# Memory attention woven between the q and output products, its two matrix products done in high and low parts

## The reference, cut to what matters

```python
def memory_cross_attention(h, mem_n, w_q, w_kv, w_o):
    q = (h @ w_q).reshape(B_, S_, MEM_HEADS, MEM_HEAD_DIM)
    kv = (mem_n @ w_kv).reshape(B_, M, 2, MEM_HEADS, MEM_HEAD_DIM)
    s = jnp.einsum('bshd,bmhd->bhsm', q, kv[:, :, 0]).astype(jnp.float32) * MEM_HEAD_DIM ** -0.5
    p = jax.nn.softmax(s, axis=-1).astype(h.dtype)
    o = jnp.einsum('bhsm,bmhd->bshd', p, kv[:, :, 1]).reshape(B_, S_, D_MODEL)
    return o @ w_o
```

## Time and profile before

| what | value |
| --- | --- |
| median of 3 runs | 3990.57 us (3990.21 to 3991.8) |
| profiled execution, its own time | 3986.77 us |
| span of its trace | 3985.5 us |
| TensorE busy | 3638.2 us, 91% of the span |
| VectorE, ScalarE, GpSimd busy | 51%, 37%, 38% |
| attention of layer 0 (first score to first matmul of the output product) | 451.66 to 498.86 us |
| the same in layer 1 | 1288.42 to 1337.18 us |

### The profile page before, as it was taken

The page is one execution under the profiler, slowest core; times in us unless marked ns, Lnnn a source line. Parts: engine busy times, 40 slices in busy tenths (PEclk is TensorE's granted clock), DMA queues, the critical chain, the costliest instruction groups (busy, mean ns, idle before and its releaser), DMA issues.

```text
span 3985.5 us, 49467 instructions
## 1 busy us (share of the span) xinstructions
PE 3638.2 (91%) x19310; PEld 2962.6 (74%) x19310; DVE 2050.4 (51%) x3613; ACT 1484.3 (37%) x2336; POOL 1529.6 (38%) x724
## 2 busy tenths in 40 slices
PE   6987889999998899988885799989999999999998
PEld 6876568887766578856773488778978888888885
DVE  3375556555445375235767419998852333323334
ACT  4544343324434333234333423337743232332222
POOL 6633224443213234433210133333444444445452
PEclk9999999999999999998985999999999999999999
DMA  5411124443212134322100124445564445444451
GB/s 190 161 56 64 43 74 148 148 148 98 70 45 95 53 112 140 98 74 72 38 3 22 43 85 127 127 127 193 206 211 146 159 131 169 139 148 158 137 160 52
DMA packets 298038, 445.36 MB, mean 112 GB/s; under 512 B 8144, under 2 KB 219088, under 8 KB 295760
## 3 DMA queue, kind: packets, MB, share of 16 engines
q1 hardware_dynamic: 278640, 371.22, 28.4%
q0 software_dynamic: 19168, 70.98, 5.5%
HBM read 383.45 MB, written 58.72 MB: 111 GB/s over the span
## 4 chain that ended last, share of the span: by engine, by line
PE 73%; DVE 16%; ACT 4%; issue 3%; POOL 2%; DMA 1%; DVEq 0%; POOLq 0%; ACTq 0%; SPq 0%
PE bank L441 21%; PE bank L443 20%; PE bank L442 20%; PE bank L2619 3%; PE bank L522 2%; DVE arena_rw L2144 2%; POOL split_low L427 2%; DVE arena L2708 1%; PE bank L1663 1%; DVE arena L2802 1%; DVE arena L2710 1%; DVE arena L2714 1%; PE bank L1687 1%; PE bank L1320 1%; PE bank L1948 1%
## 5 line engine op out<-in xcount | busy, mean ns | idle before, releaser
L427 POOL TENSOR_TENSOR split_low<-weights,split_high 128x1024 fp32r<-128x1024 f32 x554 | 1386.3, 2509 | 2150.7 <-ACT split_high L419 2150.0
L441 PE MATMUL bank<-normed_high,split_high 128*128 128x512 f32 x2480 | 991.3, 400 | 88.5 <-issue 38.8
L442 PE MATMUL bank<-normed_low,split_high 128*128 128x512 f32 x2480 | 976.5, 394 | 0.0
L443 PE MATMUL bank<-normed_high,split_low 128*128 128x512 f32 x2480 | 976.1, 394 | 0.0
L419 ACT CAST split_high<-weights 128x1024 fp32r<-128x1024 f32 x554 | 574.7, 1047 | 670.6 <-PE bank L443 575.7
L441 PEld LDWEIGHTS bank<-normed_high,split_high 128*128 128x128 f32 x2480 | 473.3, 191 | 200.0 <-issue 65.9
L441 PE MATMUL bank<-hidden_high,split_high 128*128 128x512 f32 x1536 | 601.0, 391 | 6.9 <-ACT hidden_high L2703 4.7
L443 PE MATMUL bank<-hidden_high,split_low 128*128 128x512 f32 x1536 | 599.2, 390 | 0.0
L442 PE MATMUL bank<-hidden_low,split_high 128*128 128x512 f32 x1536 | 599.0, 390 | 0.0
L442 PEld LDWEIGHTS bank<-normed_low,split_high 128*128 128x128 f32 x2480 | 473.4, 191 | 99.8 <-issue 3.4
L443 PEld LDWEIGHTS bank<-normed_high,split_low 128*128 128x128 f32 x2480 | 472.2, 190 | 100.7
(11 more groups left out here) (388 smaller groups left out, 4481.8 us busy)
## 6 DMA issues: line engine op xcount, KB each, us to landing
weights<-in_w_ff SPq DMA_DIRECT2D x64, 1024.0 KB, 5.4
weights<-in_peer_u SPq DMA_DIRECT2D x64, 1024.0 KB, 5.9
weights<-in_peer_v SPq DMA_DIRECT2D x64, 1024.0 KB, 5.0
gate_table<-arena SPq DMA_DIRECT2D x16, 2048.0 KB, 7.4
gates<-gate_table POOLq DMA_DIRECT2D x32, 1024.0 KB, 9.7
weights<-in_cond_w SPq DMA_DIRECT2D x24, 1024.0 KB, 5.3
early_table<-branch SPq DMA_DIRECT2D x72, 256.0 KB, 2.1
lates<-early_table POOLq DMA_DIRECT2D x18, 1024.0 KB, 11.1
```

Of the source, the lines that this page charges most:

```text
L427: pool.do.tensor_tensor(lo, raw_unit(u), hi.bitcast(F32), ALU.subtract).then_inc(*pool.sig("split_low", u))
L441: pe.do.matmul(o, ah, bh, start=first, stop=False)
L442: pe.do.matmul(o, ah, bl, start=False, stop=False)
L443: return pe.do.matmul(o, al, bh, start=False, stop=last)
```

## The change

The change is in the memory attention of both layers.

- The scores and the head outputs are now done by `triple`: q, k, v and the transposed probabilities get high and low parts. ScalarE casts the high parts, VectorE subtracts for the low ones. The maximum, the exponential, the inversion and the transposes stay as they are, but for the factor of -1/16 that moves into the scaling of q, so that L1369 (the scaled maximum) goes away: the minimum of the negated scores is the bias itself.
- The items start after q tile 5. A table of slots (`mem_slots`) puts q tiles 6 and 7 between the first items, and six of the eight steps of the output product's first three tiles between the later ones. A step is one channel tile for three output tiles, 9 matmuls. The last two steps and output tiles 3 to 7 follow after the items.
- The mixed result goes where q lay (`mq_high`, `mq_low`) and not into `h_hi` and `h_lo`. The buffers in SBUF move; the transposed probabilities lie in `branch`.
- In layer 1 GpSimd waits for the first tile of the mixer's output product before it fetches k and v, not for the last.

```diff
-        m_q = tiles(arena(0, CT * T), CT)
-        m_k = tiles(arena(4096, CT * M), CT)
-        m_v = arena(6144, 2 * D).rearrange("p (m c) -> p m c", m=2)
+        m_q, m_k, m_v = arena(4096, CT * T), arena(8192, CT * M), arena(12288, 2 * D)
+        mq_high, mq_low = [tiles(place(f"mem_q_{part}", A + 4096 * j, CT * T, F32R), CT)
+                           for j, part in enumerate(("high", "low"))]
...
+        MEM_LAG = 2
+
+        def mem_slots():
+            slots = [(("q", c), None) for c in range(5)]
+            slots += [(("q", 5), 0), (None, 1), (("q", 6), 2), (None, 3), (("q", 7), 4), (None, 5), (None, 6)]
+            return slots + [(("o",) if m % 2 else None, m) for m in range(7, len(MEM_ITEMS) + MEM_LAG)]
...
         def pe_mem(l):
...
+            first_o = pe_first((st, "o"), W["M", l, "o"], mq_tile, mixed(st), y_copied(st))
+            for piece, m in mem_slots():
+                if piece == ("q", 0):
+                    run(pe_first((st, "q"), ids, h_tile, h_ready(st), scaled_out((st, "q"))))
+                elif piece == ("o",):
+                    next(first_o)
+                elif piece and piece[1] >= FIRST:
+                    next(q)
+                    if piece[1] == FIRST:
+                        pe_operand_sum(st, y[:, 0, :])
+                for hd, tq in item(m):
+                    pe_mem_score(l, hd, tq)
+                for hd, tq in item(m, MEM_LAG):
+                    pe_mem_spread(l, hd, tq)
+            run(first_o)
+            pe_close(st, W["M", l, "o"], mq_tile, mixed(st), FIRST)
+
+        def pe_mem_score(l, hd, tq):
+            bank, empty = banks.take("mem_score", l, hd, tq)
+            pe.wait_ge(empty, at("mem_k_low", l))
+            for j, c in enumerate(mem_heads(hd)):
+                pe.wait_ge(at("mem_q_low", l, c))
+                last = triple(bank[:, 0:M], [t[:, tq * P:(tq + 1) * P] for t in mq_tile(c)],
+                              [t[:, c * M:(c + 1) * M] for t in (mk_high, mk_low)], j == 0, j == MEM_TILES - 1)
...
         def act_mem(l):
...
+            for piece, m in mem_slots():
+                if piece and piece[0] == "q":
+                    c = piece[1]
+                    act_split(q_unit + c + AHEAD)
+                    act.wait_ge(at("scaled_out", (st, "q"), c))
+                    act.do.copy(mq_high[:, c, :], m_q[:, c * T:(c + 1) * T]).then_inc(*act.sig("mem_q_high", l, c))
+                    if c == 3:
+                        act_mem_halves("k", l, m_k, mk_high)
+                    elif c == 5:
+                        act_mem_halves("v", l, m_v, mv_high)
...
         def dve_mem(l, before):
...
+                    dve.wait_ge(at("product", (st, "q"), c), at("root", st))
+                    dve.do.scalar_tensor_tensor(out=q32, in0=banks.tile("product", (st, "q"), c),
+                                                scalar=-(D // MEM_HEADS) ** -0.5, in1=root, op0=ALU.mult, op1=ALU.mult
+                                                ).then_inc(*dve.sig("scaled_out", (st, "q"), c))
+                    dve.wait_ge(at("mem_q_high", l, c))
+                    dve.do.tensor_tensor(mq_low[:, c, :], q32, mq_high[:, c, :].bitcast(F32), ALU.subtract
+                                         ).then_inc(*dve.sig("mem_q_low", l, c))
+                    if c == 3:
+                        dve_mem_halves("k", l, m_k, mk_high, mk_low)
+                    elif c == 5:
+                        dve_mem_halves("v", l, m_v, mv_high, mv_low)
...
-            pool.wait_ge(kv_home(l), at("product", (before, "o"), CT - 1 if before == OM else 0))
+            pool.wait_ge(kv_home(l), at("product", (before, "o"), 0))
```

More of the change, by code:

```diff
@@ L1355, in act_mem, with act_mem_halves, act_mem_out @@
             act_close(st, W["M", l, "o"])
             act_add(st, f"mlp{l}", gain_of(l, 4), 2 * W["F", l, "up", 0][0])
+        def act_mem_halves(kind, l, raw, high):
+            act.wait_ge(at(f"mem_{kind}_landed", l))
+            for i in range(2):
+                act.do.copy(high[:, i * D:(i + 1) * D], raw[:, i * D:(i + 1) * D]
+                            ).then_inc(*act.sig(f"mem_{kind}_high", l, i))
+        def act_mem_out(l, hd):
+            (high, _), empty = m_turned.take(l, hd)
+            act.wait_ge(empty, at("mem_turned", l, hd, TT - 1))
+            for mt in range(2):
+                act.do.copy(high[:, mt * T:(mt + 1) * T], banks.tile("mem_turned", l, hd, mt)
+                            ).then_inc(*act.sig("mem_turned_high", l, hd, mt))
+            m_turned.give((l, hd), ("mem_out", l, mem_heads(hd)[-1]))
+            for c in mem_heads(hd):
+                act.wait_ge(at("mem_out", l, c))
+                act.do.copy(mq_high[:, c, :], banks.tile("mem_out", l, c)
+                            ).then_inc(*act.sig("mixed_high", f"mem{l}", c))
@@ L1370, in dve_mem @@
                                          ).then_inc(*dve.sig("mem_bias", *key))
-                if 1 <= n <= len(MEM_ITEMS):
-                    key = (l,) + MEM_ITEMS[n - 1]
-                    s = small.tile("mem_soft", *key)
+                for hd, tq in item(m, 1):
+                    key = (l, hd, tq)
+                    s, pr = small.tile("mem_soft", *key), m_probs.tile(*key)
                     dve.wait_ge(at("mem_exp", *key))
@@ new lines, in dve_mem_out @@
+        def dve_mem_out(l, hd):
+            high, low = m_turned.tile(l, hd)
+            for mt in range(2):
+                half = slice(mt * T, (mt + 1) * T)
+                dve.wait_ge(at("mem_turned_high", l, hd, mt))
+                dve.do.tensor_tensor(low[:, half], banks.tile("mem_turned", l, hd, mt), high[:, half].bitcast(F32),
+                                     ALU.subtract).then_inc(*dve.sig("mem_turned_low", l, hd, mt))
+            for c in mem_heads(hd):
+                dve.wait_ge(at("mixed_high", f"mem{l}", c))
+                dve.do.tensor_tensor(mq_low[:, c, :], banks.tile("mem_out", l, c), mq_high[:, c, :].bitcast(F32),
+                                     ALU.subtract).then_inc(*dve.sig("mixed_low", f"mem{l}", c))
```

115 lines of the change are left out of this document (46 added, 69 removed).

## The result

The changed kernel takes 3998.08 us (median of 20 runs, 3993.46 to 4001.88), the kernel before 3991.17 (20 runs, 3987.45 to 4001.53). The ratio is 1.0016, 95% interval 1.001 to 1.0022: 7 us slower. That is a real loss, since the interval leaves out 1, and it is small, within the 0.2% that was called no change. The forecast was 3995.5, range 3983 to 4005. The profiled execution took 4000.11 us, its span is 3998.8.

A forecast was written before the change was run, and what follows sets the result against it. TensorE, busy 91% of the span, was taken to bound the kernel through its work and idle time. Both layers at full clock gave -4.9 us, clock falls +10; +5 on the median 3990.6 gave 3995.5 us, range 3983 to 4005.

The forecast's parts named there:

- The forecast case: Whole kernel: VectorE's low parts and the clock eat the saved passes and weaving; 3989 to 3998 us, chance 0.45.
- the slower rival: Memory attention: waits of 1.6 to 3.9 us at five paced places a layer, each followed by half clock; 3999 to 4008, chance 0.33.
- the third case: The clock holds because q and output product pieces keep TensorE busy enough; 3981 to 3989 us, chance 0.22.
- The price of the passes: TensorE's scores and head outputs: 0.72 instead of 0.86 us a score, 2.72 instead of 3.51 a head; 5.4 us saved a layer.
- The waits of layer 0: TensorE idles at scores, transposes and outputs, mostly for VectorE's low parts; 20.6 us in all against 12.8 before.
- GpSimd in the way: GpSimd's weight splits delay VectorE's low parts of q tiles 4 to 6, about 1.5 and 0.9 us for tiles 4 and 5.
- The term behind it: If GpSimd's splits also miss VectorE's subtractions, 1.9 us more a layer goes; with the clock holding, 3981.9 us.
- Layer 1: Layer 1's first score waits 1.4 us; idle time is 1.6 less than in layer 0; 3.9 us shorter at full clock.
- The clock: Five falls to half clock at ten paced places over both layers, mean 2.0 us each, 10 us; bounds 0 and +20.
- What was said to cost nothing: No cost from the removed scaled maximum, output unit 3's later split, layer 1's earlier k and v fetch, or the bank ring.
- The sum: Both layers: -4.9 us at full clock plus 10 us for the clock, so +5 us.
- Signs that failed: Expected signs: a stage ends within 4 us of before, heads take 13 us, layer 1's first wait is half layer 0's 3 us.

The follow-up runs named there:

- e11: The changed kernel with plain float32 scores, no parts of q and k, three-pass outputs, and a head's output matmuls one slot later; 3956.4 us, ratio 0.9914 to the kernel before.
- e2: The changed kernel's weave with plain float32 scores and outputs, no high and low parts of q, k, v and probabilities; 3969.2 us, ratio 0.9944 to the kernel before.
- e9: The changed kernel with three-pass scores but plain float32 outputs, without parts of v and the probabilities; 3981.7 us, ratio 0.9979 to the kernel before.
- e8: The changed kernel's weave with plain float32 scores and outputs, no parts, and a head's output matmuls one slot later; 3961.6 us, ratio 0.9927 to the kernel before.
- e5: The changed kernel with the parts of k made before the root and those of v between q tiles 6 and 7; 3990.0 us, ratio 0.9994 to the kernel before.
- e3: The changed kernel, but ScalarE splits a weight unit behind the cast of its q tile, not ahead of it; 4004.1 us, ratio 1.0033 to the kernel before.
- e14: The changed kernel with a head's output matmuls one slot later and weight units 8 to 10 split behind the exponentials; 3983.0 us, ratio 0.9978 to the kernel before.
- e1: The changed kernel's three passes and low parts without the weave: eight q tiles, then the items, then the output product; 3993.9 us, ratio 1.0008 to the kernel before.
- e15: The changed kernel with k's parts before the root, v's ahead of q tile 7, outputs one slot later, splits behind exponentials; 3965.7 us, ratio 0.9939 to the kernel before.

## Why the prediction was right

- **What bounds the stage, and the rivals.** The forecast case (saved passes and weave eaten by VectorE's low parts and the clock) came true. By the number it is a near thing: the case ended at 3998 and the slower rival began at 3999, 3998.1 lies between them, and by the mechanism it is part of the way to the rival. The clock did not hold, so the third case is out.
- **The price of the passes.** A score is 6 matmuls of 256 columns 0.12 us apart, and two scores, 12 of them, take 447.82 - 446.32 = 1.50 us; predicted 0.72 each. From the end of q tile 5 (443.57) to L522 layer 0 takes 108.0 us; less 6.3 of half clock and 17.4 of listed waits 84.3 are left, where 101.9 - 3.4 - 10.0 = 88.5 stood. So 4.2 us are saved, not 5.4 (waits too small to be listed are in both remainders). What I find of the rest is in the seams: nine matmuls of the output product take 2.17 us behind transposes (480.45 to 482.62) where I put 2.04, and a head's outputs 2.84 in e11 (470.79 to 473.63) where I put 2.72. Layer 1 by the same count (103.6 - 4.7 - 10.0 against 105.8 - 6.1 - 15.8) saves 5.0, and in layer 0 the pairs e2 and e9 (1.9 for the scores) and e8 and e11 (2.5 for the outputs) give 4.4, so the 4.2 is good to a microsecond or so. The Trainium skill (FP8 and Floating Point Precision, TensorE Precision Notes), by whose four passes a quarter would be saved, was the worse guide: 6.9 by its rule, 5.4 by rows, 4.2 to 5.0 measured.
- **The waits of layer 0.** Predicted 3.0, 1.9, 3.9, 1.7, 2.1, twice 2.45, 0.9, 1.6; measured 2.59, 1.64, 3.36, 1.32, 1.84, twice 2.22, 0.83, 1.40, each in its place. The releasers are those named, but for the first: its record says only "issue", and that it is the low part of k shows in VectorE's order (its two subtractions end at 446.22) and in e5, where k is ready early and the wait is gone. The tile cycle is 1.98 us, not 2.07, and that is in all of them. The sum was 20.6 with small waits, and the listed ones are 17.4: 3 us too much, against TensorE's 1.2 too little. At full clock 100.9 was predicted and 108.0 - 6.3 = 101.7 measured.
- **GpSimd in the way.** Right as a mechanism (1.53, 1.54 and 2.42 us for tiles 4, 5 and 6), though the row of 2.73 that I called a subtraction (L565) is an addition, of two SBUF operands too. The term behind it, 1.9 us a layer if the splits missed the low parts, was not to be had by e3 or e14: in e3 GpSimd met other instructions, in e14 the next unit met the same one.
- **Layer 1.** Here I was off. I expected 1.4 us at the first score and it is 2.61 as in layer 0. Before, q tiles behind the sum ran at half clock in layer 1, so q tile 5 ended 10.5 us behind the root; after, it ended 8.7 behind it (1276.74 to 1285.44), and VectorE's 11.5 us from the root to the low part of k were uncovered to that extent. So the faster q tiles came back as 1.2 us of wait, which my sum, counted from the end of q tile 5, did not have.
- **The clock.** Close, and in part by luck. I took five falls of ten places that set the pace, 2.0 us each, 10 in all. The trace has six there, 2.4 + 2.5 + 1.4 and 1.6 + 1.5 + 1.4, 10.8 us. But five of ten was a share, not a mechanism, and like waits were followed by half clock and not (last section); each place more or less is 1.4 to 2.5 us. The seventh, 1.6 us at the first score of layer 1, was hidden as said: TensorE came to the first transposes so much later that no wait was left there, where layer 0 waited 1.64.
- **What was said to cost nothing** did: no wait at output tile 3 for its split, none for k and v in layer 1.
- **The sum.** From the end of q tile 5 layer 0 is 108.0 - 101.9 = 6.1 us longer and layer 1 105.8 - 103.6 = 2.2; 8.3 against a predicted 5.1, and 6.9 us by the medians. The 3.2 us between are 0.8 in layer 0 at full clock (101.7 for 100.9), 1.6 in layer 1 (105.8 - 4.5 = 101.3 for 99.7) and 0.8 of the clock. Counted from the root the two stages are only 6.4 us longer, which fits the medians: in layer 1 the q tiles up to tile 5 came 1.8 us sooner (10.5 to 8.7), which was in no term of mine. So the distance of 2.6 us from the forecast is in part luck.
- **Signs that failed.** No stage was to end more than 4 us from before, and layer 0's is 5.9 us longer; heads were to take 13 us and took 15 to 16 with half clock in them; the first wait of layer 1 was to be half of layer 0's and is as long.

What the prediction did not weigh is what the kernel could have been. Taken in that order the weave gives 22 us and the passes and parts take 29. They don't simply add: without the weave the same passes and parts cost 2.6 us (e1), and with them in place the weave costs 4.2 (e1 against the change). The 29 us are what the parts cost once the weave has put them where TensorE waits for them. I had no row that priced the weave apart from the parts, and e2 alone shows it.

## What to carry to other kernels

When a change moves little, run each of its parts without the others: here a gain of 22 us was hidden. One such run is not enough, since the passes and parts alone looked harmless (2.6 us) and cost 29 on top of the weave. Work that feeds a product which is waited for belongs ahead of what releases it, or a slot away from its use: moving a head's outputs one slot later was worth 17 us with no arithmetic changed. A cheaper matmul is paid for by whoever makes its operands; here it pays for the outputs once their parts are hidden (e11 against e8), and in none of these arrangements for the scores, whose parts stand in the chain behind the root (e9, e15).

## What the runs showed of the hardware

- GpSimd's subtraction of two SBUF operands holds up some instructions of VectorE for as long as it runs, and not others. A scaling from SBUF to SBUF of 0.35 us took 2.35 and a subtraction of two SBUF operands of 0.69 took 2.42, ending 0.15 and some 0.5 us behind GpSimd's 2.34 and 2.35; L1406, which reads a bank and an SBUF tile, kept its 0.68 us at 446.14 beside GpSimd. The size of the loss is about what is left of GpSimd's instruction, not a share of one's own. The Trainium skill (SBUF — State Buffer, Who interferes with whom) calls this an exclusive lock, and these rows agree. Working in SBUF is not enough to be held up: far behind the two layers this search for maxima, with one operand in SBUF, keeps its 0.27 us in the middle of a subtraction on GpSimd.

```profile
2401.58 0.27 DVE L2771 MAX8 arena<-arena 128x8 f32<-128x128 f32 x1
```

```profile
2400.12 2.40 POOL L427 TENSOR_TENSOR split_low<-weights,split_high 128x1024 fp32r<-128x1024 f32 x1 [7.04 <-ACT split_high L419]
```

- The same idle time is not always followed by half clock. Behind 2.22 us it came at 490.14 and not at 505.12 in the same stage; behind 3.07 us at the sum of layer 1 it did not come after the change, and behind 3.08 at the same place before the change it did. In the six stages whose waits ahead of matmuls are at most 1.5 us (e2, e8, e11) the granted clock is 1.00 throughout. But before, a wait of 1.25 us was followed by it. What decides between like waits stays open here.
